# The gates' steps of a delta-rule layer between other dense products on TensorE, ScalarE and VectorE

## The reference

```python
proj = h @ w_in
qkv = jax.nn.silu(causal_depthwise_conv(proj[..., :3 * GDN_WIDTH], conv_w))
z = proj[..., 3 * GDN_WIDTH:4 * GDN_WIDTH].reshape(B, T, GDN_HEADS, GDN_HEAD_DIM)
a = proj[..., 4 * GDN_WIDTH:4 * GDN_WIDTH + GDN_HEADS]
b = proj[..., 4 * GDN_WIDTH + GDN_HEADS:]
q, k, v = split(qkv, 3)
q = l2norm(q) * GDN_HEAD_DIM ** -0.5
k = l2norm(k)
beta = jax.nn.sigmoid(b)
g = -jnp.exp(a_log) * jax.nn.softplus(a + dt_bias)
o = chunk_gated_delta_rule(q, k, v, g, beta)
```

## Time and profile before

| | us |
|---|---|
| median of 3 runs | 2766.74 |
| lowest and highest | 2765.53, 2769.02 |
| span of the profiled execution, first to last instruction | 2753.5 |
| median less that span | 13.2 |
| TensorE busy | 2565.5 |
| VectorE busy | 1268.5 |
| ScalarE busy | 876.8 |
| GpSimd busy | 449.1 |
| mean granted clock of TensorE (1 is full speed, 2.4 GHz) | 0.954 |

### The profile page before, as it was taken

One profiled execution on the slowest core, in us unless ns is written; L12 is line 12 of the kernel. 1 busy time (PEld: TensorE's weight loads), 2 busy tenths in 40 slices (PEclk: granted clock), 3 DMA queues, 4 the chain that ended last, 5 costly groups with the idle time before them and its releaser, 6 DMA issues.

```text
span 2753.5 us, 33730 instructions
## 1 busy us (share of the span) xinstructions
PE 2565.5 (93%) x13381; PEld 2024.9 (74%) x13381; DVE 1268.5 (46%) x2164; ACT 876.8 (32%) x1572; POOL 449.1 (16%) x467
## 2 busy tenths in 40 slices
PE   7899989999899997997799999998989899999998
PEld 6799987666665555885468888876977877788887
DVE  6876844323321112414447675354746654433333
ACT  3354445422211112325533222234222323322222
POOL 4654604000123221300010000000300300100001
PEclk9899989999899997999899999998989999999999
DMA  5443402033369995320026575231012002332322
GB/s 180 151 123 115 153 28 82 20 92 111 154 257 404 412 407 202 100 85 1 0 77 194 177 219 159 73 89 39 1 31 62 1 22 75 88 95 84 112 77 77
DMA packets 315085, 332.44 MB, mean 121 GB/s; under 512 B 20848, under 2 KB 273904, under 8 KB 302512
## 3 DMA queue, kind: packets, MB, share of 16 engines
q1 hardware_dynamic: 292720, 281.73, 31.3%
q0 software_dynamic: 22208, 48.55, 5.2%
HBM read 372.15 MB, written 16.78 MB: 141 GB/s over the span
## 4 chain that ended last, share of the span: by engine, by line
PE 53%; DVE 4%; ACT 3%; issue 1%; DMA 0%; POOL 0%; ACTq 0%; DVEq 0%; POOLq 0%
PE bank L493 11%; PE bank L495 11%; PE bank L494 11%; PE bank L3181 5%; PE bank L2725 1%; PE bank L403 1%; PE bank L405 1%; PE bank L404 1%; PE bank L756 1%; PE bank L3264 1%; PE bank L3257 1%; PE bank L3251 1%; PE bank L2571 1%; PE bank L2570 1%; PE bank L2572 1%
## 5 line engine op out<-in xcount | busy, mean ns | idle before, releaser
L348 DVE TENSOR_TENSOR sb_w_lo<-sb_weights,sb_w_hi 128x1024 fp32r<-128x1024 f32 (+2 forms) x221 | 246.8, 1127 | 447.9 <-ACT sb_w_hi L342 447.9
L493 PE MATMUL bank<-sb_h_hi,sb_w_hi 128*128 128x512 f32 x1040 | 422.6, 406 | 8.0 <-DVE sb_w_lo L348 8.0
L494 PE MATMUL bank<-sb_h_lo,sb_w_hi 128*128 128x512 f32 x1040 | 409.4, 394 | 0.0
L495 PE MATMUL bank<-sb_h_hi,sb_w_lo 128*128 128x512 f32 x1040 | 409.2, 393 | 0.0
L342 ACT CAST sb_w_hi<-sb_weights 128x1024 fp32r<-128x1024 f32 x224 | 215.5, 969 | 505.1 <-PE bank L495 438.1
L493 PEld LDWEIGHTS bank<-sb_h_hi,sb_w_hi 128*128 128x128 f32 x1040 | 197.6, 190 | 63.5 <-issue 22.3
L494 PEld LDWEIGHTS bank<-sb_h_lo,sb_w_hi 128*128 128x128 f32 x1040 | 197.8, 190 | 45.7 <-issue 5.3
L495 PEld LDWEIGHTS bank<-sb_h_hi,sb_w_lo 128*128 128x128 f32 x1040 | 197.4, 190 | 43.0
L544 POOL TENSOR_TENSOR sb_scratch<-sb_scratch 128x512 f32<-128x512 f32 x30 | 38.5, 1285 | 1142.5 <-ACT sb_scratch L534 1142.5
L403 PE MATMUL bank<-sb_wide,sb_h_hi 128*128 128x512 f32 (+2 forms) x448 | 179.3, 400 | 11.2 <-DVE sb_wide L385 7.0
L404 PE MATMUL bank<-sb_wide,sb_h_hi 128*128 128x512 f32 (+2 forms) x448 | 172.9, 386 | 0.0
(11 more groups left out here) (557 smaller groups left out, 4710.6 us busy)
## 6 DMA issues: line engine op xcount, KB each, us to landing
sb_weights<-ffn_w_in SPq DMA_DIRECT2D x88, 512.0 KB
sb_weights<-w_in SPq DMA_DIRECT2D x52, 512.0 KB
sb_xT<-ada_w POOLq DMA_DIRECT2D x24, 1024.0 KB, 6.8
sb_weights<-ada_w SPq DMA_DIRECT2D x24, 1024.0 KB
sb_expert_weights<-w_down SPq DMA_DIRECT2D x22, 1024.0 KB
sb_expert_weights<-w_gate SPq DMA_DIRECT2D x20, 1024.0 KB
sb_expert_weights<-w_up SPq DMA_DIRECT2D x19, 1024.0 KB
sb_weights<-ffn_w_out SPq DMA_DIRECT2D x32, 512.0 KB
```

What stands on the lines that cost most here:

```text
L348: dve.tensor_tensor(u.lo[:, 0:u.kt, :], u.chunk.w, u.hi[:, 0:u.kt, :].bitcast(F32), ALU.subtract).then_inc(*k.lo.one())
L493: pe.matmul(bank[:], u.hi[:, kk, :], act[0][:, kk, :], start=first and kk == 0, stop=False)
L494: pe.matmul(bank[:], u.hi[:, kk, :], act[1][:, kk, :], start=False, stop=False)
L495: mm = pe.matmul(bank[:], u.lo[:, kk, :], act[0][:, kk, :], start=False, stop=last and kk == u.kt - 1)
```

## The change

The steps run at other turns. On TensorE steps 1, 2, 3 stood behind products 1, 3 and 6, and now stand behind 1, 2 and 8. On ScalarE steps 2, 3, 4 stood in turns 2, 4, 8, and now in 1, 3, 9. On VectorE steps 2, 3, 4 stood in turns 3, 5, 7 (the fourth `next` only ends the generator, in turn 9), and now in 2, 5, 8, with the same end in turn 9. No instruction is added or taken away, and no operand or semaphore is changed.

```diff
@@ channels_pe
                 split_product_pe(k, units[s], h, k.bank[s % 4])
-        if s in (1, 3, 6):
+        if s in (1, 2, 8):
             next(other, None)
         n = s - 3
@@ channels_act
             split_hi_act(k, u)
-        if s in (2, 4, 8):
+        if s in (1, 3, 9):
             next(other, None)
         n = s - 4
@@ channels_dve
             split_lo_dve(k, u)
-        if n in (3, 5, 7, 9):
+        if n in (2, 5, 8, 9):
             next(other, None)
         if n == 5:
```

## The result

The changed kernel took 2746.6 us in the median of 7 runs (2745.8 to 2750.2), the kernel before, run beside it, 2765.5 (2755.0 to 2769.0): a ratio of 0.994 (95% interval 0.9923 to 0.9957), some 19 us in the medians. Forecast were 7.0 us and a range of 2757.0 to 2763.5: the sign was right, the size was not, and the time lies outside the range.

A forecast was written before the change was run, and what follows sets the result against it. TensorE, busy for nearly all of the span, was taken as the bound. Terms 0.97 + 3.12 + 2.06 + 1.79 - 0.2 = 7.7, less 0.9, gave 6.8; TensorE's sequence 7.9 - 0.9 = 7.0: 2759.7 us, range 2757.0 to 2763.5.

The forecast's parts named there:

- First wait: TensorE's idle time at the transposes of the gate rows, for ScalarE's copy: shrinks by 0.97 to 1.97 us.
- Clock behind it: TensorE's half clock after the gate-row transposes: its 3.12 us cost goes, less 0.9 for a possible fall.
- Rival 1: Clock after the gate-row transposes falls as far as before, costing 3.1 us: gain 4.8, time 2761.9; chance 0.14.
- Second wait and its clock: TensorE's idle time for VectorE's cumulative decays goes, 2.06 us saved, and the half clock after it, 1.79 saved.
- What is late next: TensorE waits about 0.2 us for ScalarE's copy of the turned keys before channel 6's transposes; no product waits for weights.
- Rival 2: ScalarE's long step of four table loads holds the loop; at doubled load cost gain 2.6, time 2764.1; chance 0.06.
- The sum: Savings in the changed stage: 7.7 us, or 7.9 by TensorE's sequence, less 0.9 for the clock; 7.0 taken.
- TensorE's order: Second count along TensorE's sequence: product 7 ends 8.5 us earlier, less 0.3 and 0.2, 8.0 before the clock deduction.
- everything from channel 11 on keeps its distances: Work from channel 11 of the changed stage onward was taken as unchanged in spacing, with no gain or loss.
- the first reading: Median 2766.7 against profiled span 2753.5: about 13.2 us taken to lie outside the span, unchanged.
- Rival 3: TensorE stays at half clock through the rest of the changed stage: 11.6 us slower, 2778, if through products 3 to 8; chance 0.03.

The follow-up runs named there:

- the first half: Only step 2 moved (TensorE behind product 2, ScalarE turn 1, VectorE turn 2) against the kernel before: 2761.3 us, ratio 0.9986.
- this half: Only steps 3 and 4 moved (TensorE behind product 8, ScalarE turn 9, VectorE turn 8) against the kernel before: 2755.1 us, ratio 0.9972.

## Why the prediction was right or wrong

**First wait.** Right: 1.97 forecast, 1.98 measured, one product earlier.

**Clock behind it.** I took 0.9 us for a fall behind the wait that stays. It cost nothing: the clock was 1.00 in the changed kernel, its repeats and the kernel with the first half alone. So Rival 1 is out. Length alone does not decide: the wait of 2.06 us before, with the gates' and the query rows' small products behind it, was followed by 0.50. Full products on both sides may be the reason; where the wait lies against the clock's changes was not varied here, so the cause is not shown.

**Second wait and its clock.** Right. Alone this half saved 3.7 us in the stage; 2.06 + 1.79 = 3.85 was the sum.

**What is late next.** The copy of the turned keys was to cost 0.2 us and cost none: it was over at 1895.46, and TensorE came to the transposes behind product 9 only at 1896.27. ScalarE's long step took 6.2 us, with table loads of 1.28 each, as in the earlier trace rows; Rival 2 is out. The drain that the Trainium skill's page "ScalarE: Activation LUTs" (section "What ACT_TABLE_LOAD costs") adds to a load is not in this trace either: the load at 1861.24 ends at 1862.52 and the next operation starts at 1862.53.

**The sum.** For the stage 7.9 without the clock's deduction, measured 7.4. TensorE's order gave 8.5 us up to the end of product 7 and the profiles have 8.0: a channel with its small product took 6.73 us there (1854.44 to 1861.17 in the changed kernel) and not 5.66 + 0.96 = 6.62. The 0.9 deducted for a fall that did not come nearly makes up for it. That the two profiled spans differ by 7.6, close to the forecast 7.0, is partly luck: 7.4 in the stage, 1.2 in the first chunks and second channels and 1.2 in the rest, less 2.2 for a later start.

**The step that failed** is "everything from channel 11 on keeps its distances": a term put at nothing with no row behind it. The runs have 9.8, 12.4 and 18.9 us where 7.0 was forecast. With the waits in the tails of both chunk stages filled, only 4.9 and 3.6 us are left between the two kernels, so some 5 us or more of the unfilled gain hang on half clock in those tails. The filling took 16 to 18 us off the kernel before. In the profiles the first chunk stage went from 124.3 to 124.5 down to 123.6 to 123.8, the second channels from 91.5 or more to 91.1 or less, and the second chunk stage from 129.4 (119.1 in the odd first profile) to 126.9 and 127.0 (119.2 in the first). How the rest of the 18.9 us of the first measurement splits between the tail, the scatter ahead of the stage and the chip is open; that measurement has one profile of each kernel, and that of the kernel before was not a usual one. The times do not tell the clock in the tail by themselves: of the changed kernel's 19 runs 13 were at 2751.1 or less, of the 108 of the kernel before 7 were under 2757, but one of the 13 (2751.0) was profiled with the clock lost in its tail.

**What hid it** is the first reading: "about 13.2 us lie outside the span; I take them as unchanged and subtract from the median". Outside the span lie 1.2 us. The other 12 were inside the spans of the timed runs and not in the profiled one; in the repeat that was profiled 10.3 of them are in the second chunk stage (129.4 against 119.1). This reading puts no wrong term into the forecast gain, but a median 12 us over a profiled span was the sign that the profile was of an unusual execution. The long half clock of the second tail is missing from it; that at the end of the first chunk stage is there, and was not looked for (windows view of the kernel before):

```profile
2040.00:2062.00 22.00, 18.42 (x67) 15.29 (x68) 8.52 (x12) 5.75 (x6) 0.00 (x0) 0.61 0.37 96
```

Rival 3 had half clock that outlasts small waits, but in the changed kernel's stage and as a loss. It was found 300 us further on, in both kernels, and costs the changed one less.

**Open.** Why the clock falls at one restart and not at another. The same restart of the changed kernel lay 416.94 us behind the first product of the changed stage in one profile, which kept its clock, and 416.88 and 416.94 in two, which lost it. Measured from the fall ahead of the stage it is 420.1 against 419.8 in both others, so a difference in place of 0.3 us is not excluded. My rule for it was refuted.

## What to carry to other kernels

Compare the profiled span with the timed median first. Here each run's own time was 1.2 or 1.3 us over its span, so a gap of 12 us meant that the profile was of another kind of execution than the median. Take a second profile of the same kernel then, before any sum is made.

In this kernel a stretch of small products with waits of 1.3 us and more between them is where the clock was lost in most profiles, and not in all. Filling such waits with products that nobody reads is worth trying: here 14 fills in two tails, 7 us of added work, took 16 to 18 us off the kernel before. Its runs then spread over 2 us, where those of the kernel before beside it spread over 7.

When a saving upstream gives far more or far less than itself, try the same delay with idle work: if fills of 1 to 3 us change the time by 7, part of the gain is position, and the next change of any length may take it back. Of eight such delays here two did so clearly. Of the five aimed at the tail from profiles four missed their forecast, so a shift can show the effect but could not be aimed.

## What the runs showed of the hardware

The granted clock fell in small products behind a wait of 1.31 us (from 2251.3, 0.50 for 27 us), and did not behind a wait of 1.98 us between full products (1.00 from 1848.3 to 1888.1). So the length of a wait alone does not decide. The wait of 1.31 us itself was followed by a fall in one profile and not in another of the same program. Half clock held for 27 us while TensorE was busy for 24 of them; in the changed kernel's repeat it came in two stretches of 10 and 14 us.

A table load of ScalarE took 1.28 us, and the next operation started 0.01 us behind it.

The kernel's time changed by 7 us when idle work was put in some 300 us ahead of the second chunk stage's tail: 2.7 us of it made the kernel before faster, 0.8 us made the changed kernel slower.
